# Two changes to a two-block transformer kernel: layer loops written out, and channel sums placed one half lot later

## The chip, the cores and the metric

The kernel runs on one core of a Trainium2 chip, in one launch. The metric is device time in microseconds (us), the median of the runs. The core has a matrix engine (TensorE, PE; its weight loads are shown apart as PEld), three engines for elementwise work (VectorE, DVE; ScalarE, ACT; GpSimd, POOL) and SyncE (SP), which here starts most DMA transfers. Each engine runs its own instruction stream; they meet through semaphores only.

## The reference

Two different transformer blocks of two layers each run one after the other on 512 tokens of width 1024 in fp32. The first has 16 leading meta tokens, so it works on 528.

```python
for l in range(2):                        # first block, 528 tokens
    z = rms_norm(h) @ w_in                # q, k, v, forget logit, a_val, a_gate, sc_b, sc_c, sc_x
    y_attn = forgetting_attention(q, k, v, log_sigmoid(f_logit + b))
    a = a_val * sigmoid(a_gate)
    a = causal_depthwise_conv(a, a_dw_w) + a_dw_b      # 31 taps, 256 channels
    y_conv = silu(layer_norm(a)) @ a_pw_w              # mean and variance over the 256 channels
    y_sc = sc_b * causal_depthwise_conv(sc_c * sc_x, sc_conv_w)   # 3 taps
    h = h + rms_norm(head_rms_norm([y_attn, y_conv, y_sc]) @ w_out)
    h = h + rms_norm((silu(g) * up) @ w_down)          # g, up: causal conv of rms_norm(h) @ w_up
for l in range(2):                        # second block, 512 tokens
    x = x + [stick_breaking, moba, nsa, diff attention](rmsnorm(x) @ w_in) @ w_out
    x = x + square(relu(rmsnorm(x) @ w_up)) @ w_down
```

## The kernel before

Activations stay in SBUF with the features on the 128 partitions and the tokens along the row. Each fp32 operand of a large product is split into a high and a low part, and a product is three matmuls (`product`: L156, L157, L159). Weights come in tiles of 2048 columns into a ring of two slots (SP, L1211 in the input stage). For each lot of weights ScalarE makes the high part (`weight_high`, L140) and VectorE the low part (`weight_low`, L147).

A layer is a chain of stages. Each stage is one `nc.Block`: a program per engine, with a barrier of all engines behind it. Inside, every engine works in the order in which its code is written; only semaphores tie them together. A `Signal` counts per layer, and its `at(layer, n)` gives the value to wait for: `layer * (per_layer * step) + n * step`. The layers of each block are a loop on the chip (`nc.Fori(0, DEPTH)`, L2012 and L3288), so `layer` is a register, and each such wait needs its value worked out in a register first. There are further loops inside the stages, such as TensorE's over lots (L1241, L1713, L241) and those of the helper `in_rounds` (L176) on ScalarE, VectorE and GpSimd.

The change is in the input stage of the first block (`in_stage_a`). TensorE works there through
- 11 lots of branch weights (gates, values, short convolution, forget logit),
- 8 lots of query and key weights, in a loop of 2 × 4 (L1241),
- the channel sums of the long convolution (`channel_sums(acc)`, four matmuls at L1252), which wait for all taps,
- 4 lots of value weights: two pairs, `s` = 0 and 1, each with a first and a second `half` of the 8 contraction steps. For each half, five token tiles of 4 products are accumulated in five PSUM banks (`V_BANKS`); between the pairs stand the channel sums of the squares (`channel_sums(gate)`), and behind them the pointwise product (L1287).

VectorE does the 31 taps of the long convolution on two groups of channels (L1403), spread between the lots, the last 32 of its 62 steps in the loop over query and key lots. Behind the channel sums it centres the result (L1464), does the forget gate's running sum (L1472), the low part of the third value lot, the short convolution (L1481 to L1490), the low part of the fourth, and the scaling by the root (L1502). ScalarE squares the centred result (L1345), makes the high part of the third value lot, copies the values of the first pair out of PSUM (L1309), makes the high part of the fourth, and takes the logarithm, the root and the silu (L1356, L1359, L1364).

The taps' wait is in front of the value lots, so these stand behind it although they don't need the convolution:

```python
pe.wait_ge(dve_step.sem, dve_step.at(layer, M["steps"]["conv"]))
channel_sums(acc)
for s in range(2):
```

At the start of the input stage TensorE adds 2 to its own count of done lots; ScalarE's first weight copy (L140) waits for it.

Of the kernel before, what the change touches and what calls it, by code (L numbers as in the profile page):

```python
# [9 lines left out]

# [18 lines left out]
DEPTH = 2  # L31
# [28 lines left out]
class Signal:  # L60


    def __init__(self, sem, per_layer, step=1):
        self.sem, self.per_layer, self.step = sem, per_layer, step
# [29 lines left out]
class Scope:  # L94


    def __init__(self, nc, ctx):
        self.nc, self.ctx = nc, ctx

    def sb(self, name, shape, dtype=F32):  # L100
        return self.ctx.enter_context(self.nc.sbuf_tensor(name, shape, dtype))

    def parts(self, name, *shape):
# [1064 lines left out]
def in_stage_a(nc, S, G, W, layer, A, M, h):  # L1168
# [5 lines left out]
    act_out, dve_out, dve_step, f_step = S["act_out"], S["dve_out"], S["dve_step"], S["f_step"]  # L1174
# [6 lines left out]
    mm0, QK, V, N_LOTS = 2, 11, 19, 23  # L1181
# [20 lines left out]
    with nc.Block() as block:  # L1202
# [11 lines left out]
        def _(pe):  # L1214
# [33 lines left out]
            def channel_sums(x):  # L1248

                for j in range(2):  # L1250
                    for c, (c0, cn) in enumerate(chunks(TA)):
                        mm = nc.tensor.matmul(ps[:, 6 + c, 0:cn], S["mean256"][:, :], x[:, j, c0:c0 + cn],  # L1252
                                              start=(j == 0), stop=(j == 1))
                mm.then_inc(ln_pe.sem, 1)


            pe.wait_ge(dve_step.sem, dve_step.at(layer, M["steps"]["conv"]))
            channel_sums(acc)
            for s in range(2):
                for half in range(2):  # L1260
                    p = V + 2 * s + half
                    pe.wait_ge(w_lo.sem, w_lo.at(layer, p + 1))
                    for i, (q0, _) in enumerate(K_TILES_A):
                        if half == 0 and (s == 1 or i >= 2):

                            pe.wait_ge(act_out.sem, act_out.at(layer, 15 + i if s else 13 + (i >= 4)))
                            if s == 0:
                                pe.wait_ge(qk_low.sem, qk_low.at(layer, 9 + (i >= 4)))
                        for k in range(4):
                            kk, cols = 4 * half + k, slice(k * 256, (k + 1) * 256)  # L1270
                            mm = product(nc, [ps[:, V_BANKS[i], 0:256]],
                                         tuple(w[:, kk * TA + q0:kk * TA + q0 + P] for w in u_wide),
                                         [(W["hi"][:, p % 2, cols], W["lo"][:, p % 2, cols])],
                                         kk == 0, kk == KD - 1)
                        mm.then_inc(mm_done.sem, 1)
                if s == 0:

                    pe.wait_ge(ln_act.sem, ln_act.at(layer, 2))
                    channel_sums(gate)
# [617 lines left out]
def first_stack(nc, G, A, h):  # L1897

    with ExitStack() as ctx:
# [109 lines left out]
            glu_stage_a(nc, S, G, W, D, layer, A, M, hid, h)  # L2009
            layer_end_a(nc, S, G, layer, A, y, h, col("ffn_post"))  # L2010

        with nc.Fori(0, DEPTH) as layer:  # L2012
            with ExitStack() as whole:
                held = Scope(nc, whole)
                pads = held.sb("y_a", [P, 4 * (TA + TAPS_SHORT - 1) + 4 * TA])
                W = weight_parts(held, "w_a")
                y = part(pads, 0, KD, TA)
                with ExitStack() as inner:
                    mixer(layer, Scope(nc, inner), y, W)
                with ExitStack() as inner:  # L2020
                    glu(layer, Scope(nc, inner), y, pads, W)
# [1130 lines left out]
def second_stack(nc, G, A, h_all, out):  # L3152

    h = h_all[:, :, META:TA]
    with ExitStack() as ctx:
# [129 lines left out]
                             needs=(S["sq_out"], (20 + 8, 20 + 16)), stats=1, free="down_free", bank=4)]  # L3285
            mlp_stage_b(nc, S, G, W, layer, A, ups, downs, col("mlp_g"), u, relu, hid, h)

        with nc.Fori(0, DEPTH) as layer:  # L3288
            with ExitStack() as inner:
                mixer(layer, Scope(nc, inner))  # L3290
            with ExitStack() as inner:
                mlp(layer, Scope(nc, inner))
# [233 lines left out]
```

## Time and profile before

| what | value |
|---|---|
| median of 3 runs | 3087.64 us (3073.48 to 3090.52) |
| the profiled execution: its time, its span | 3083.47 us, 3081.7 us |
| instructions in the profile | 48063 |
| mean granted TensorE clock | 0.949 of full speed |
| first block, layer 0 and layer 1 | 26 to 772 us, 772 to 1523 us |
| second block, layer 0 and layer 1 | 1527 to 2294 us, 2294 to 3073 us |

The span is the time from the first to the last instruction of the profile. "Busy" leaves out register, branch and semaphore instructions; these are shown on an engine's queue (PEldq, DVEq, ACTq) in the views by source line. The granted clock is TensorE's: 1.00 is 2.4 GHz and 0.50 is 1.2 GHz. A row in order of time gives the start, the duration, what ran, and in brackets how long the engine was idle before it and what ended this; a merged row "x8" holds eight records (each of the four matmuls of the channel sums leaves two).

### The profile page before, as it was taken

The page shows a single profiled execution, that of the slowest core. Times are in us where ns is not written, and L with a number is a line of the kernel's source. Part 1 is how long each engine was busy: PE and PEld are TensorE (multiplying, and loading weights), DVE is VectorE, ACT ScalarE, POOL GpSimd, SP SyncE. Part 2 cuts the span into 40 slices and gives each one's busy share as a digit, 9 for nine tenths or more (in the row PEclk, how much of TensorE's full clock was granted, in tenths as well). Part 3 has the DMA queues.
Part 4 walks back from the last instruction along what each step waited for, and adds up shares of the span by engine and source line. Part 5 has one row for each costly group of instructions (what it writes and reads, how often), then busy time and mean ns, then how long its engine had stood idle before and what let it go on. Part 6 is the DMA issues. An engine that isn't in the chain of part 4 may idle for free. (4 is left out here: it accounts for less than half of the span.)

```text
span 3081.7 us, 48063 instructions
## 1 busy us (share of the span) xinstructions
PE 2867.3 (93%) x18250; PEld 2459.6 (80%) x18250; DVE 1435.9 (47%) x2287; ACT 1069.1 (35%) x1486; POOL 236.5 (8%) x210
## 2 busy tenths in 40 slices
PE   7988899999889989999898889999989888999998
PEld 6977899998887789999787556788868754578886
DVE  3633477732563367772333554433433255443343
ACT  3234433322224443332333333422323333343232
POOL 1001300010100120001100022000010001200001
PEclk9989999999998899999899889999999988899999
DMA  3200322222210132222322001222222200122223
GB/s 126 90 28 15 130 82 95 77 95 74 89 69 14 42 117 95 82 91 95 111 100 92 28 1 44 92 96 96 96 88 96 96 28 1 42 82 95 96 96 109
DMA packets 44806, 238.20 MB, mean 77 GB/s; under 512 B 4895, under 2 KB 14751, under 8 KB 21361
## 3 DMA queue, kind: packets, MB, share of 16 engines
q1 hardware_dynamic: 34976, 223.04, 20.9%
q10 hardware_dynamic: 9680, 13.17, 1.3%
q8 instruction: 94, 1.54, 0.2%
q14 instruction: 56, 0.45, 0.0%
HBM read 234.04 MB, written 11.59 MB: 80 GB/s over the span
## 5 line engine op out<-in xcount | busy, mean ns | idle before, releaser
L156 PE MATMUL psum<-u_up_a_hi,w_a_hi 128*128 128x264 f32 x1408 | 378.7, 289 | 19.2 <-DVE u_up_a_lo L1882 15.8
L157 PE MATMUL psum<-u_up_a_lo,w_a_hi 128*128 128x264 f32 x1408 | 374.5, 286 | 0.0
L147 DVE TENSOR_TENSOR w_mlp_b_lo<-ring,w_mlp_b_hi 128x1024 fp32r<-128x1024 f32 x128 | 157.0, 1226 | 330.3 <-ACT w_mlp_b_hi L140 330.3
L147 DVE TENSOR_TENSOR w_a_lo<-ring,w_a_hi 128x1024 fp32r<-128x1024 f32 (+1 forms) x154 | 187.7, 1220 | 227.8 <-ACT w_a_hi L140 225.4
L156 PEld LDWEIGHTS psum<-u_up_a_hi,w_a_hi 128*128 128x128 f32 x1408 | 266.1, 189 | 26.8 <-DVE u_up_a_lo L1882 19.6
L159 PE MATMUL psum<-u_up_a_hi,w_a_lo 128*128 128x264 f32 x1408 | 286.9, 285 | 0.0
L140 ACT ACTIVATE w_a_hi<-ring 128x1024 fp32r<-128x1024 f32 (+1 forms) x154 | 161.4, 1049 | 308.2 <-PE psum L159 303.0
L157 PEld LDWEIGHTS psum<-u_up_a_lo,w_a_hi 128*128 128x128 f32 x1408 | 265.8, 189 | 0.4
L140 ACT ACTIVATE w_mlp_b_hi<-ring 128x1024 fp32r<-128x1024 f32 x128 | 135.6, 1060 | 299.6 <-PE psum L159 298.8
L159 PEld LDWEIGHTS psum<-u_up_a_hi,w_a_lo 128*128 128x128 f32 x1408 | 220.4, 190 | 0.0
L156 PE MATMUL psum<-u_up_b_hi,w_mlp_b_hi 128*128 128x512 f32 x512 | 200.9, 392 | 9.7 <-DVE u_up_b_lo L489 9.7
L157 PE MATMUL psum<-u_up_b_lo,w_mlp_b_hi 128*128 128x512 f32 x512 | 200.6, 392 | 0.0
L159 PE MATMUL psum<-u_up_b_hi,w_mlp_b_lo 128*128 128x512 f32 x512 | 200.3, 391 | 0.0
L156 PE MATMUL psum<-hid_b_hi,w_mlp_b_hi 128*128 128x512 f32 x512 | 199.2, 389 | 0.0
L159 PE MATMUL psum<-hid_b_hi,w_mlp_b_lo 128*128 128x512 f32 x512 | 199.2, 389 | 0.0
L157 PE MATMUL psum<-hid_b_lo,w_mlp_b_hi 128*128 128x512 f32 x512 | 199.2, 389 | 0.0
L156 PE MATMUL psum<-u_in_a_hi,w_a_hi 128*128 128x264 f32 x608 | 167.2, 294 | 28.5 <-DVE u_in_a_lo L1419 19.6
L157 PE MATMUL psum<-hid_a_lo,u_up_a_hi 128*128 128x264 f32 x660 | 173.9, 284 | 0.0
L156 PE MATMUL psum<-hid_a_hi,u_up_a_hi 128*128 128x264 f32 x660 | 173.3, 283 | 0.0
L157 PE MATMUL psum<-u_in_a_lo,w_a_hi 128*128 128x264 f32 x608 | 165.6, 291 | 0.0
L1856 DVE SCALAR_TENSOR_TENSOR y_a<-y_a,cols_a 128x528 f32<-128x528 f32 x176 | 135.3, 769 | 25.3 <-DVE y_a L1856 11.9
L156 PEld LDWEIGHTS psum<-u_in_a_hi,w_a_hi 128*128 128x128 f32 x608 | 118.6, 195 | 31.9 <-DVE u_in_a_lo L1419 21.3
(452 smaller groups left out, 6551.0 us busy)
## 6 DMA issues: line engine op xcount, KB each, us to landing
ring<-in_wup SPq DMA_DIRECT2D x44, 1024.0 KB, 4.8
ring<-in_wup_b SPq DMA_DIRECT2D x32, 1024.0 KB, 4.8
ring<-in_wdown_b SPq DMA_DIRECT2D x32, 1024.0 KB, 4.9
ring<-in_win SPq DMA_DIRECT2D x22, 1024.0 KB, 4.8
ring<-in_wdown SPq DMA_DIRECT2D x32, 704.0 KB, 4.0
ring<-in_win_b SPq DMA_DIRECT2D x12, 1024.0 KB, 4.8
near_copies<-near_rows ACTq DMA_DIRECT2D x2, 4608.0 KB
ring<-in_wout SPq DMA_DIRECT2D x8, 1024.0 KB, 4.8
```

Source lines behind the costliest of these rows:

```text
L140: nc.scalar.activation(W["hi"][:, buf, 0:n], W["tiles"][:, slot, at:at + n], ACT.Copy).then_inc(W["w_hi"].sem, 1)
L147: nc.vector.tensor_tensor(W["lo"][:, buf, 0:n], W["tiles"][:, slot, at:at + n], W["hi"][:, buf, 0:n].bitcast(F32), ALU.subtract).then_inc( ...
L156: nc.tensor.matmul(out[c], a_hi, b_hi, start=start, stop=False)
L157: nc.tensor.matmul(out[c], a_hi, b_lo, start=False, stop=False)
L159: mm = nc.tensor.matmul(out[c], a_lo, b_hi, start=False, stop=stop)
L1856: nc.vector.scalar_tensor_tensor(out=cv[:, j, :], in0=z_pad[:, j, tap:tap + TA], scalar=wcol[tap], in1=cv[:, j, :], op0=ALU.mult, op1=ALU. ...
```

## The change

There are two edits. The layer loops of both blocks become loops of the source: each layer's code is written out, and `layer` is a number. A tile name would then be used twice, so `Scope.sb` adds a number to it. And `channel_sums(acc)` with its wait is placed behind the first half of the first value pair. The other engines' code stays as it is.

```diff
 class Scope:
+    used = collections.Counter()
     def sb(self, name, shape, dtype=F32):
+        self.used[name] += 1
+        name = name if self.used[name] == 1 else f"{name}_{self.used[name]}"
         return self.ctx.enter_context(self.nc.sbuf_tensor(name, shape, dtype))
...
-
-            pe.wait_ge(dve_step.sem, dve_step.at(layer, M["steps"]["conv"]))
-            channel_sums(acc)
             for s in range(2):
                 for half in range(2):
                     p = V + 2 * s + half
+                    if p == V + 1:
+
+                        pe.wait_ge(dve_step.sem, dve_step.at(layer, M["steps"]["conv"]))
+                        channel_sums(acc)
                     pe.wait_ge(w_lo.sem, w_lo.at(layer, p + 1))
...
-        with nc.Fori(0, DEPTH) as layer:      # first block
+        for layer in range(DEPTH):
...
-        with nc.Fori(0, DEPTH) as layer:      # second block
+        for layer in range(DEPTH):
```

TensorE in the input stage, before: the end of the loop over query and key lots, the channel sums (matmuls of `mean`, which is 1/256 everywhere), and the start of the first value pair (its stationary operand is the activation, so the names stand the other way round).

```order
L159 MATMUL psum<-u_in_a_hi,w_a_lo 128x264 x2
L1241 REGISTER_ALU
L1241 COMPARE_AND_BRANCH
L1257 ISA
L1252 MATMUL psum<-arena_a,mean 128x264 [waits dve_step]
L1252 MATMUL psum<-arena_a,mean 128x264 x3
L1262 REGISTER_ALU
L156 MATMUL psum<-w_a_hi,u_in_a_hi 128x256 [waits w_lo_a]
L157 MATMUL psum<-w_a_lo,u_in_a_hi 128x256
```

After, the end of the same loop with what follows it, and the place of the sums 60 matmuls on (lines of the changed kernel are 5 or 6 higher):

```order
L164 MATMUL psum<-u_in_a_hi,w_a_lo 128x264 x2
L1246 REGISTER_ALU
L1246 COMPARE_AND_BRANCH
L161 MATMUL psum<-w_a_hi,u_in_a_hi 128x256 [waits w_lo_a]
L162 MATMUL psum<-w_a_lo,u_in_a_hi 128x256
```

```order
L164 MATMUL psum<-w_a_hi,u_in_a_lo 128x256
L1257 MATMUL psum<-arena_a,mean 128x264 [waits dve_step]
L1257 MATMUL psum<-arena_a,mean 128x264 x3
L161 MATMUL psum<-w_a_hi,u_in_a_hi 128x256 [waits w_lo_a]
L162 MATMUL psum<-w_a_lo,u_in_a_hi 128x256
```

The value lot follows the loop at once, the sums stand between its two halves, and the register instructions in front of the waits are gone.

VectorE at the end of a layer of the first block, before: the last residual additions, the barrier, and the loop's jump back to the input stage.

```order
L580 TENSOR_TENSOR h<-h,y_a 128x528 [waits res_scaled]
L567 UNCONDITIONAL_BRANCH
L2012 REGISTER_ALU [waits barrier_Pool_Activation_PE_DVE_SP_release]
L2012 COMPARE_AND_BRANCH
L3288 UNCONDITIONAL_BRANCH [waits barrier_Pool_Activation_PE_DVE_SP_release]
```

After, the end of layer 0 and the start of layer 1:

```order
L585 TENSOR_TENSOR h<-h,y_a 128x528 [waits res_scaled] x2
L572 UNCONDITIONAL_BRANCH
L1381 UNCONDITIONAL_BRANCH [waits barrier_Pool_Activation_PE_DVE_SP_release]
L1415 MEMSET arena_a 128x2x30
L1416 MEMSET arena_a 128x2x2
```

The jump is gone and the next layer's first operation stands straight behind the barrier. TensorE has 4634 rows in its program before and 8607 now, VectorE 1410 and 1829; the loops inside the stages are kept.

## Rows read from the trace of the kernel before

**Rows 1.** The page: busy time and share of each engine.
```profile
PE 2867.3 (93%) x18250; PEld 2459.6 (80%) x18250; DVE 1435.9 (47%) x2287; ACT 1069.1 (35%) x1486; POOL 236.5 (8%) x210
```

**Rows 2.** TensorE in order of time: start us, us, line, operation, [idle before].
```profile
154.43 0.40 PE L159 MATMUL psum<-u_in_a_hi,w_a_lo 128*128 128x264 f32 x2
...
160.57 3.88 PE L1252 MATMUL psum<-arena_a,mean 128*128 128x264 f32 x8 [5.74 <-DVE arena_a L1403]
...
179.08 1.94 PE L1252 MATMUL psum<-arena_a,mean 128*128 128x264 f32 x8
...
180.66 0.47 PE L156 MATMUL psum<-w_a_hi,u_in_a_hi 128*128 128x256 f32 x1
...
194.94 0.28 PE L159 MATMUL psum<-w_a_hi,u_in_a_lo 128*128 128x256 f32 x1
...
908.35 3.89 PE L1252 MATMUL psum<-arena_a,mean 128*128 128x264 f32 x8 [5.74 <-DVE arena_a L1403]
...
926.74 1.94 PE L1252 MATMUL psum<-arena_a,mean 128*128 128x264 f32 x8
```

**Rows 3.** Stretches: us, busy of PE, PEld, DVE, ACT, POOL, granted clock, DMA.
```profile
160.50:165.60 5.10, 5.03 (x15) 4.20 (x16) 1.12 (x3) 0.36 (x1) 0.00 (x0) 0.50 0.17 72
...
200.30:291.60 91.30, 82.69 (x519) 63.34 (x519) 33.76 (x120) 40.05 (x82) 11.39 (x14) 0.83 0.00 1
...
948.00:1043.20 95.20, 86.94 (x519) 66.99 (x519) 33.70 (x120) 40.04 (x82) 11.41 (x14) 0.78 0.00 1
...
1728.90:1884.90 156.00, 140.72 (x1014) 82.46 (x1014) 84.50 (x282) 56.28 (x89) 28.91 (x24) 0.86 0.00 1
...
2500.50:2663.30 162.80, 147.09 (x1014) 84.95 (x1014) 84.56 (x282) 56.27 (x89) 28.91 (x24) 0.82 0.00 1
```

**Rows 4.** ScalarE and VectorE in order of time, around the moved step.
```profile
155.84 0.59 ACT L1340 ACTIVATE qk_hi<-psum 128x528 f32 x1
...
157.11 0.70 DVE L1453 SCALAR_TENSOR_TENSOR qk_lo<-psum,qk_hi 128x528 f32 x1
...
164.50 1.32 DVE L1464 TENSOR_TENSOR arena_a<-arena_a,psum 128x528 f32<-128x528 f32 x2 [3.98 <-PE psum L1252]
...
172.18 1.06 ACT L140 ACTIVATE w_a_hi<-ring 128x1024 fp32r<-128x1024 f32 x1 [5.68 <-PE psum L159]
```

**Rows 5.** All engines in order of time, at the four input stages' starts.
```profile
25.55 1.04 ACT L1138 ACTIVATE fixed_a<-fixed_a_staged 128x1024 fp32r<-128x1024 f32 x1
...
32.28 0.59 PE L156 MATMUL psum<-u_in_a_hi,w_a_hi 128*128 128x264 f32 x1 [8.05 <-DVE u_in_a_lo L1419]
...
770.48 0.64 ACT L559 ACTIVATE rstd<-rstd 128x528 f32<-128x528 f32 x1
...
774.61 0.11 DVE L1409 MEMSET arena_a<- 128x60 f32 x1 [7.05 <-issue]
...
780.26 0.59 PE L156 MATMUL psum<-u_in_a_hi,w_a_hi 128*128 128x264 f32 x1 [10.54 <-DVE u_in_a_lo L1419]
...
1524.49 1.72 ACTq L2094 DMA_DIRECT2D strips<-near_copies  x1
...
1531.78 0.79 PE L156 MATMUL psum<-u_in_b_hi,w_in_b_hi 128*128 128x512 f32 x1 [10.03 <-DVE u_in_b_lo L2251]
...
2293.88 0.63 ACT L327 ACTIVATE rstd<-rstd 128x512 f32<-128x512 f32 x1
...
2303.64 0.80 PE L156 MATMUL psum<-u_in_b_hi,w_in_b_hi 128*128 128x512 f32 x1 [10.52 <-DVE u_in_b_lo L2251]
```

**Rows 6.** Loop branches by line: count, ns min/median/max, first and last start.
```profile
L2012 PEldq COMPARE_BRANCH  x2: 78/1895/3712, 771.6 to 1523.8; - x2
...
L1713 PEldq COMPARE_BRANCH  x20: 76/212/220, 408.1 to 1374.8; - x20
...
L176 DVEq COMPARE_BRANCH  x52: 49/56/78, 394.9 to 3048.5; - x52
```

**Rows 7.** ScalarE in order of time, layer end: the operation ahead of 770.48.
```profile
769.75 0.70 ACT L556 ACTIVATE rstd<-psum,eps 128x528 f32<-128x528 f32 x1 [1.52 <-PE psum L547]
```

More of the change, by code:

```diff
@@ L13 @@
+import collections
 from contextlib import ExitStack, nullcontext
```

## The prediction

> **What bounds the kernel now.** I read four views: the page for the busy shares, then TensorE's rows in order of time around the moved step, then the stretches with their granted clock, and last the rows on both sides of each stage boundary. In the page TensorE is busy for 93% of the span and no other engine for half of it [rows 1], so an edit is worth what it takes out of TensorE's idle time or gives back of its clock. Two places are touched.
>
> The first is the long convolution of the input stage. TensorE ends its last query/key lot at 154.43 + 0.40 = 154.83 us, waits 5.74 us for VectorE's last tap, computes the channel sums from 160.57 us, and then has value work up to the next channel sums at 179.08 us [rows 2]. It runs at the lower of its two clock levels, 1.2 GHz, from 160.5 to 165.6 us: the stretch shows a granted clock of 0.50 [rows 3]. So the wait is paid twice, as idle time and as slow work behind it. Layer 1 repeats it: wait 5.74 us, sums from 908.35 us, next sums at 926.74 us [rows 2].
>
> The second is the edge between the two layers of each block. From the last operation of the stage ahead to TensorE's first matmul of the input stage there are, in the first block, 32.28 − 26.59 = 5.69 us at layer 0 (the operation starts at 25.55 us and takes 1.04 us) but 780.26 − 771.12 = 9.14 us at layer 1. In the second block they are 1531.78 − 1526.21 = 5.57 us (from the end of a DMA issue of 1.72 us that starts at 1524.49 us) and 2303.64 − 2294.51 = 9.13 us [rows 5]. The work after the boundary is the same; only the later ones are reached by the loop's jump back. TensorE's branch there takes 3.712 us once (taken) and 0.078 us once (loop left) [rows 6].
>
> **The change part by part.** *The sums behind the first half.* The step issues four 264-column matmuls per layer and one wait; nothing else moves, no DMA, and SP's and GpSimd's rows do not hold it. TensorE's row becomes: first half of the first value lots (60 matmuls), wait for the taps, four matmuls, second half. At full clock the four take 180.66 − 179.08 = 1.58 us, and two halves take 194.94 + 0.12 − 180.66 = 14.40 us (lots of the same shape in the second pair, 0.12 us from matmul to matmul) [rows 2]. Each half is then 7.20 us, longer than the 5.74 us that are to be filled: it would end at 162.0 us, when the tap that ended the wait (at about 160.5 us) is 1.5 us old, so the moved wait costs nothing.
>
> Before, from 160.57 to 179.08 us, 18.51 us; at full clock 1.58 + 14.40 = 15.98 us. Gain in layer 0: 5.74 + 18.51 − 15.98 = 8.27 us. In layer 1: 5.74 + (926.74 − 908.35) − 15.98 = 8.15 us. Together 16.4 us. The 2.5 us of clock in each agree with half of the 5.1 us at 0.50 [rows 3].
>
> Can the first half start 5.74 us earlier? Its weights' low part is made in the loop ahead. Its fifth tile writes the bank that the last query/key lot is read from: ScalarE reads it at 155.84 us and VectorE at 157.11 + 0.70 = 157.81 us [rows 4], while the fifth tile is only due at 154.83 + 4 × 1.44 = 160.6 us. Covered by 2.8 us; without this cover the wait would come back before tile 5.
>
> What is queued behind the sums? VectorE's centring starts at 164.50 us now [rows 4]; then it would start with the end of the sums, 162.0 + 1.6 + some 0.3 = 163.9 us, so no later. ScalarE's squares end some 2 us on, at 166 us, and TensorE's next sums need them at 154.83 + 15.98 = 170.8 us: 5 us of room where there were 13. ScalarE's copy of the next weights stands behind those squares. Today it starts at 172.18 us [rows 4], when the first half frees its buffer; then the squares release it at about 166 us, VectorE's low part follows by 168.5 us, and TensorE asks for it at 170.8 + 1.6 = 172.4 us: 4 us of room. From there each step keeps its distance to TensorE's, and the stage's end moves forward whole.
>
> *The layer loops in the source.* Both jumps back go, and layer 1 is entered straight on as layer 0 is: (9.14 − 5.69) + (9.13 − 5.57) = 3.45 + 3.56 = 7.0 us. VectorE shows it too: its first operation of layer 1 starts at 774.61 us, 3.49 us behind ScalarE's last [rows 5]. Inner loops stay loops, and they already jump back without such a stall: TensorE's in the gated unit take 0.076 to 0.220 us, VectorE's 0.049 to 0.078 us over 52 of them [rows 6]. The price is a program for each engine nearly twice as long.
>
> The Trainium skill, "Runtime: NRT & Kernel Launch", Instruction fetch mechanics, says that a taken branch whose target is not in the held window of two 16 KiB pages waits for its code to be fetched. It names no price; the 3.712 us is this case's row. The Trainium skill, "Advanced Engine Details and Errata", Control Flow Timing, gives about 108 ns for a compare-and-branch and speaks against a gain: by it the two jumps are worth an estimated 0.2 us, and the sum would be 16.6 us instead of 23.4 us. The trace bears it out for inner loops and contradicts it for the layer's.
>
> *Waits on constants.* With the layer known, waits outside the inner loops need no register arithmetic. Where the trace shows such a wait it costs nothing: the table operation that starts at 769.75 us and takes 0.70 us is followed, over a wait on a register, 0.03 us later [rows 5, 7]. That is the lower end, 0. The upper end is by the nearest row that bears a price per wait, VectorE's loop branch with at most 0.078 us [rows 6]: if some 100 handoffs of the attention stages lost as much, 7.8 us. A loss has no carrier, since nothing is added. I take 0, as in the row of the wait itself.
>
> *What no row fixes.* The attention stages run the same code in both layers and take different times, as their clock falls differently: 91.3 and 95.2 us in the first block (0.83 and 0.78), 156.0 and 162.8 us in the second (0.86 and 0.82) [rows 3]. The change moves all four in time by 8 to 23 us, so each may land on either figure: −3.9 or +3.9 in the first block, −6.8 or +6.8 in the second, a range of ±10.7 us, middle 0.
>
> **The sum.** 16.4 + 7.0 = 23.4 us. Against the profiled execution, 3083.47 us, that gives 3060 us (span 3081.7 − 23.4 = 3058.3 us, and 1.8 us around it). Its median of runs was 4.2 us higher, 3087.64 us, which gives 3064 us. I forecast 3062 us.
>
> **The rivals.** *A: the jump's price returns.* The fetch is not avoided but shifts to the entry of layer 1, because its code was never loaded before. For it: half of each program is new code. Against it: layer 0's entries are new code too and cost 5.6 us. Then 16.4 us are left: 3083.5 to 3087.6 − 16.4, about 3070 us.
>
> *B: the sums' wait moves instead of going.* If the chain of centring, squares and weights were 5 us longer than worked out, TensorE would wait at the next sums for the 8 us gained, and only the loops' 7.0 us stay: about 3079 us. Against it: the 4 and 5 us of room above, from rows at either end.
>
> *C: slower, by inner loops that no longer stay loaded.* The duplicated code stands at other addresses. If the long loop of the gated unit (9 jumps back per layer, bodies of 24 us) lay so that its start is dropped before the jump, each jump would cost TensorE 3.7 us as the layer's did: 18 × 3.5 = 63 us, and the time 3062 + 63 = 3125 us. From 7 such jumps on (7 × 3.5 = 24.5 us) it eats the gain. Against it: 20 branches there with a maximum of 0.220 us [rows 6], and the bodies keep their length. The Trainium skill's section on instruction fetch, named above, would allow this for a body that leaves the window.
>
> *D: the clock's draw.* All four attention stages on their slow side: the gain shrinks by 10.7 us, to 3073 us.
>
> **How the numbers follow.** Forecast 0.68, A 0.10, B 0.08, C 0.04, D 0.10. A measurement of this kernel tells about 0.5% (15.4 us) from no change, so "faster" ends at 3072.2 us. The forecast gives 0.66 of faster, A half, D half, B none; with some room for what I do not see: faster 0.80, within 0.16, slower 0.04. The range takes in the two scales (3060 and 3064), the upper end of the constants (−7.8), the clock's draw both ways and A and D: 3046 to 3077 us. B's end and C lie outside, about 0.1.
>
> **What would show it.** The wait of 5.74 us at the convolution's sums is gone in both layers, or is under 0.5 us, and no granted clock of 0.50 stands behind it; the next sums start about 16 us behind the last query/key lot, without a new wait. The branch of 3.7 us is absent, and the first matmul of layer 1 comes 5.5 to 6 us behind the stage ahead in both blocks. Wrong would be: a wait for squares or weights in the value lots (B), 9 us at layer 1's entry (A), inner branches above 1 us (C), or attention stages that all take longer (D).

## The result, and the profile after

The changed kernel takes 3052.66 us, the median of 6 runs (3048.62 to 3057.41); the kernel before takes 3081.34 us in 6 runs on the same chip (3073.48 to 3090.52). The ratio is 0.9904, with a 95% interval of 0.988 to 0.9928, so it is faster clear of the noise, by about 1%. The forecast was 3062 us in a range of 3046 to 3077 us. The span fell from 3081.7 to 3055.6 us and the instructions from 48063 to 45807. Lines of the changed kernel are 5 or 6 higher than those of before.

The page of the changed kernel, busy time of each engine: TensorE does the same 18250 matmuls in nearly the same busy time as in [rows 1], in a shorter span.

```profile
PE 2866.0 (94%) x18250; PEld 2463.7 (81%) x18250; DVE 1437.4 (47%) x2287; ACT 1068.1 (35%) x1486; POOL 236.4 (8%) x210
```

TensorE of the changed kernel in order of time, around the moved sums (L1257 now, L161 to L164 are the products). It answers to [rows 2].

```profile
154.05 0.40 PE L164 MATMUL psum<-u_in_a_hi,w_a_lo 128*128 128x264 f32 x2
154.29 0.28 PE L161 MATMUL psum<-w_a_hi,u_in_a_hi 128*128 128x256 f32 x1
...
161.38 1.94 PE L1257 MATMUL psum<-arena_a,mean 128*128 128x264 f32 x8
...
170.26 1.95 PE L1257 MATMUL psum<-arena_a,mean 128*128 128x264 f32 x8
...
894.97 1.94 PE L1257 MATMUL psum<-arena_a,mean 128*128 128x264 f32 x8
...
903.85 1.95 PE L1257 MATMUL psum<-arena_a,mean 128*128 128x264 f32 x8
```

There is no bracket in front of either sum: both waits of 5.74 us are gone, and so is the slow clock behind them, since the first sums take 1.94 us for their eight records, as the second do, instead of 3.88 us. The same in stretches (columns as in [rows 3]): the first half lot, then the sums and the second half.

```profile
154.20:161.30 7.10, 7.10 (x63) 7.10 (x62) 4.62 (x7) 1.56 (x2) 0.00 (x0) 1.00 0.46 148
...
161.38:170.26 8.88, 8.88 (x71) 8.62 (x69) 6.86 (x10) 3.76 (x11) 0.00 (x0) 1.00 0.01 2
```

ScalarE and VectorE behind the sums, which answer to [rows 4]: the squares are made from 164.10 us and end at 164.10 + 1.26 = 165.36 us, 4.9 us ahead of the sums over them, and the copy of the next weights starts at 165.27 us instead of 172.18 us.

```profile
164.10 1.26 ACT L1351 ACTIVATE arena_a<-arena_a 128x528 f32<-128x528 f32 x2 [8.06 <-DVE arena_a L1470]
165.27 1.04 ACT L145 ACTIVATE w_a_hi<-ring 128x1024 fp32r<-128x1024 f32 x1
...
163.36 1.32 DVE L1470 TENSOR_TENSOR arena_a<-arena_a,psum 128x528 f32<-128x528 f32 x2 [3.23 <-PE psum L1257]
...
166.50 1.19 DVE L152 TENSOR_TENSOR w_a_lo<-ring,w_a_hi 128x1024 fp32r<-128x1024 f32 x1
```

The four entries of an input stage, ScalarE's last operation ahead of each and TensorE's first matmul. They answer to [rows 5] (in the second block's first entry the DMA issue on ACTq is the one ahead).

```profile
26.67 1.04 ACT L1143 ACTIVATE fixed_a<-fixed_a_staged 128x1024 fp32r<-128x1024 f32 x1
...
33.23 0.56 PE L161 MATMUL psum<-u_in_a_hi,w_a_hi 128*128 128x264 f32 x1 [7.88 <-DVE u_in_a_lo L1425]
...
759.97 0.64 ACT L564 ACTIVATE rstd<-rstd 128x528 f32<-128x528 f32 x1
...
761.05 0.11 DVE L1415 MEMSET arena_a<- 128x60 f32 x1 [4.58 <-PEq L572]
...
766.15 0.56 PE L161 MATMUL psum<-u_in_a_hi,w_a_hi 128*128 128x264 f32 x1 [6.95 <-DVE u_in_a_lo L1425]
...
1496.14 0.45 ACTq L2100 DMA_DIRECT2D strips<-near_copies  x1
...
1502.42 0.77 PE L161 MATMUL psum<-u_in_b_hi,w_in_b_hi 128*128 128x512 f32 x1 [8.87 <-DVE u_in_b_lo L2257]
...
2264.63 0.63 ACT L332 ACTIVATE rstd<-rstd 128x512 f32<-128x512 f32 x1
...
2270.53 0.76 PE L161 MATMUL psum<-u_in_b_hi,w_in_b_hi 128*128 128x512 f32 x1 [6.66 <-DVE u_in_b_lo L2257]
```

Layer 1 is entered in 766.15 − 760.61 = 5.54 us in the first block (9.14 before) and in 2270.53 − 2265.26 = 5.27 us in the second (9.13 before): 3.60 + 3.86 = 7.46 us. Layer 0's entries take 5.52 and 5.83 us, about as before. VectorE's first operation of layer 1 comes 0.44 us behind ScalarE's last, where it was 3.49 us. The layer's branch is gone from the trace.

How the branch of before got onto the path takes a second look, since TensorE itself had nothing to do in its 3.7 us. ScalarE's first weight copy of the stage waits until TensorE has added to its count (L1232). The branch starts at 771.6 us and takes 3.712 us, so it ends at 775.3 us, and the copy follows:

```profile
775.52 1.06 ACT L140 ACTIVATE w_a_hi<-ring 128x1024 fp32r<-128x1024 f32 x1 [4.40 <-PEq L1232]
```

VectorE's low part, and with it TensorE's first matmul at 780.26 us, stand behind this copy. In the changed kernel the copy starts at 761.11 us, 0.5 us behind ScalarE's last operation. TensorE's branch is not the whole delay: ScalarE and VectorE, too, went on only at 774.4 us before, so a quick branch on TensorE alone would have won about 1 us (an estimate, 775.5 − 774.5). And what goes on meanwhile shows in the DMA queues: from 771.5 to 775.3 us, while TensorE stands in the branch, the queues of instructions move five packets.

```profile
q14 instruction: 4, 0.03, 2.9%
q8 instruction: 1, 0.02, 2.1%
```

At the second block's jump (2294.9 to 2298.6 us) they move three. In the same stretches of the changed kernel, 760.8 to 764.6 us and 2265.4 to 2269.1 us, they move none.

The attention stages and the short stick-breaking ahead of the second block's attention, in stretches; the first four answer to [rows 3].

```profile
191.60:282.60 91.00, 83.10 (x519) 63.78 (x519) 33.82 (x120) 39.99 (x82) 11.43 (x14) 0.83 0.00 1
925.20:1017.20 92.00, 84.08 (x519) 64.46 (x519) 34.03 (x120) 40.05 (x82) 11.43 (x14) 0.81 0.00 1
1702.80:1856.30 153.50, 138.16 (x1014) 83.12 (x1014) 85.45 (x282) 56.13 (x89) 28.83 (x24) 0.87 0.00 1
2470.80:2635.20 164.40, 148.92 (x1014) 87.64 (x1014) 85.63 (x282) 56.23 (x89) 28.83 (x24) 0.81 0.00 1
1641.20:1702.80 61.60, 46.33 (x240) 26.59 (x240) 28.04 (x61) 20.24 (x33) 0.00 (x0) 0.84 0.20 68
```

The stage of the last row took 58.2 us at a clock of 0.91 before:

```profile
1670.70:1728.90 58.20, 43.30 (x240) 24.61 (x240) 28.03 (x61) 20.24 (x33) 0.00 (x0) 0.91 0.21 73
```

### Where the 26 us of the span are

From barrier to barrier of the two traces, in us; "written out" and "moved" are the two single edits of the experiments below.

| stage | before | after | moved | written out |
|---|---|---|---|---|
| input, first block, layer 0 | 173.6 | 163.8 | 164.1 | 171.1 |
| input, first block, layer 1 | 176.7 | 164.4 | 168.6 | 169.8 |
| gated unit, layers 0 and 1 | 410.5, 410.5 | 408.3, 408.6 | 410.5, 410.5 | 408.4, 408.7 |
| input, second block, layer 1 | 147.9 | 144.0 | 147.7 | 144.0 |
| attention, first block | 91.2, 95.2 | 91.0, 92.0 | 91.4, 90.3 | 87.8, 87.8 |
| stick-breaking, second block | 58.2, 57.9 | 61.5, 61.5 | 59.5, 59.6 | 61.4, 61.4 |
| attention, second block | 156.1, 162.9 | 153.5, 164.4 | 162.8, 159.2 | 150.5, 164.4 |

Input stages give 9.9 + 12.3 + 3.9 us, the gated unit 4.1 us. The stages of the last three rows together lose some 2.3 us, and the other stages differ by less than 1.5 us each.

### The profile page after: what moved, and what is told of

Its sections match the earlier page's. It is cut to its first block and busy times, and to the rows that moved or that the text cites. A ratio compares the mean times of both kernels' runs of the same rounds, so it can differ in the third digit from the quotient of the medians.

```text
span 3055.6 us, 45807 instructions
## 1 busy us (share of the span) xinstructions
PE 2866.0 (94%) x18250; PEld 2463.7 (81%) x18250; DVE 1437.4 (47%) x2287; ACT 1068.1 (35%) x1486; POOL 236.4 (8%) x210
## 5 line engine op out<-in xcount | busy, mean ns | idle before, releaser
L161 PE MATMUL psum<-u_up_a_hi,w_a_hi 128*128 128x264 f32 x1408 | 378.6, 289 | 15.6 <-DVE u_up_a_lo L1888 15.4
L164 PE MATMUL psum<-u_up_a_hi,w_a_lo 128*128 128x264 f32 x1408 | 287.0, 285 | 0.0
L161 PEld LDWEIGHTS psum<-u_up_a_hi,w_a_hi 128*128 128x128 f32 x1408 | 266.1, 189 | 22.4 <-issue 14.6
L164 PEld LDWEIGHTS psum<-u_up_a_hi,w_a_lo 128*128 128x128 f32 x1408 | 220.5, 190 | 0.0
L161 PE MATMUL psum<-u_up_b_hi,w_mlp_b_hi 128*128 128x512 f32 x512 | 201.6, 394 | 9.7 <-DVE u_up_b_lo L494 9.7
L164 PE MATMUL psum<-u_up_b_hi,w_mlp_b_lo 128*128 128x512 f32 x512 | 200.9, 392 | 0.0
L161 PE MATMUL psum<-hid_b_hi,w_mlp_b_hi 128*128 128x512 f32 x512 | 199.3, 389 | 0.0
L164 PE MATMUL psum<-hid_b_hi,w_mlp_b_lo 128*128 128x512 f32 x512 | 199.2, 389 | 0.0
L161 PE MATMUL psum<-u_in_a_hi,w_a_hi 128*128 128x264 f32 x608 | 166.9, 293 | 23.4 <-DVE u_in_a_lo L1425 15.0
L161 PE MATMUL psum<-hid_a_hi,u_up_a_hi 128*128 128x264 f32 x660 | 173.3, 283 | 0.0
L1862 DVE SCALAR_TENSOR_TENSOR y_a<-y_a,cols_a 128x528 f32<-128x528 f32 x176 | 135.3, 769 | 24.3 <-DVE y_a L1857 6.1
L152 DVE TENSOR_TENSOR w_in_b_lo<-ring,w_in_b_hi 128x1024 fp32r<-128x1024 f32 x48 | 59.3, 1235 | 173.8 <-ACT w_in_b_hi L2195 173.8
```

What stands on the lines that cost most here:

```text
L152: nc.vector.tensor_tensor(W["lo"][:, buf, 0:n], W["tiles"][:, slot, at:at + n], W["hi"][:, buf, 0:n].bitcast(F32), ALU.subtract).then_inc( ...
L161: nc.tensor.matmul(out[c], a_hi, b_hi, start=start, stop=False)
L164: mm = nc.tensor.matmul(out[c], a_lo, b_hi, start=False, stop=stop)
L1862: nc.vector.scalar_tensor_tensor(out=cv[:, j, :], in0=z_pad[:, j, tap:tap + TA], scalar=wcol[tap], in1=cv[:, j, :], op0=ALU.mult, op1=ALU. ...
```

## The experiments

### One edit at a time

First the sums' move alone: the changed kernel with both layer loops back on the chip.

```diff
-        for layer in range(DEPTH):
+        with nc.Fori(0, DEPTH) as layer:      # both blocks
```

> The sums behind the first half of the first value lots, with the layer loops left on the chip. Theory (two separate gains that add up): the wait of 5.74 us per layer and the slow clock behind it go, 16.4 us, so the ratio to the kernel before is about 0.9947; the two jumps of 3.7 us stay, and an iteration of the gated unit's long loop stays at 23.95 us. Rival (the written-out layers are what makes room for the moved sums, as fewer register instructions stand ahead of the waits): a new wait shows at the next channel sums or in the value lots, and less than 10 us are gained.

Measured: 3068.09 us, ratio 0.9953 (0.9926 to 0.9981). The sums stand at full clock without a wait, close to the ratio of 0.9947 that was expected. The layers' branches are back: TensorE's taken one takes 3.918 us in the first block (the row below) and 3.456 us in the second.

```profile
L1257 PE MATMUL psum<-arena_a,mean x32: 386/386/387, 162.3 to 912.3; 128*128 128x264 f32 x32
...
L2018 PEldq COMPARE_BRANCH  x2: 67/1992/3918, 763.8 to 1502.5; - x2
```

Then the loops alone: the changed kernel with the sums at their old place.

```diff
+            pe.wait_ge(dve_step.sem, dve_step.at(layer, M["steps"]["conv"]))
+            channel_sums(acc)
             for s in range(2):
...
-                    if p == V + 1:
-                        pe.wait_ge(dve_step.sem, dve_step.at(layer, M["steps"]["conv"]))
-                        channel_sums(acc)
```

> The layers written out, with the channel sums at their old place. Theory: 7.0 us from the two entries, some 4 us from the gated unit's long loop (23.95 us an iteration before, 23.73 us in the changed kernel), ratio about 0.9965; the wait of 5.74 us and the clock of 0.50 behind it stay in both layers. Rival (the jump's price returns at the entry of layer 1, or the long loop is faster for the place of its code alone and not for this part): first matmul of layer 1 about 9 us behind the stage ahead, ratio 0.999 to 1.001.

Measured: 3067.86 us, ratio 0.9953 (0.9931 to 0.9974); the expected 0.9965 lies inside the interval. The wait is there, 5.74 us to the hundredth, in both layers. Layer 0:

```profile
158.99 3.66 PE L1257 MATMUL psum<-arena_a,mean 128*128 128x264 f32 x8 [5.74 <-DVE arena_a L1407]
...
176.68 1.95 PE L1257 MATMUL psum<-arena_a,mean 128*128 128x264 f32 x8
```

What follows: by the whole times the edits are additive as far as these can tell. 0.9953 × 0.9953 = 0.9906, and both together measured 0.9904. The table shows most of each gain in its own stages: the move's in the first block's input stages (9.5 and 8.1 us), the loops' in the two entries of layer 1 and, which I had not forecast, in the gated unit, which falls by 2 us per layer only where the layers are written out.

Stage by stage the traces add up less well. The loops alone also shorten the first block's input stages by 2.5 and 6.9 us (3.6 us of the latter are the entry), while on top of the move they give only 0.3 and 4.2 us. Most of the difference is the clock: in the trace of the loops alone the wait of 5.74 us is followed by 17.69 and 17.71 us up to the next sums instead of 18.51 and 18.39 us, and behind the wait for the forget logit in layer 1 the clock did not fall at all.

```profile
843.20:851.20 8.00, 7.94 (x65) 7.94 (x66) 2.95 (x5) 5.63 (x7) 0.00 (x0) 1.00 0.35 126
```

So what the slow clock adds to one and the same wait is not a fixed sum: behind 5.74 us it was 1.7 us in this trace (17.69 − 15.98) and 2.5 us in that of the kernel before.

### The wait's idle time and the clock behind it

The kernel before, with 44 matmuls of no use in front of the taps' wait, so that TensorE is busy there and the rest of the program stays as it is.

```diff
+            pe.wait_ge(w_lo.sem, w_lo.at(layer, V + 1))
+            for n in range(44):
+                nc.tensor.matmul(ps[:, V_BANKS[0], 0:256], u_wide[0][:, n % 4 * TA:n % 4 * TA + P],
+                                 W["hi"][:, V % 2, n % 4 * 256:(n % 4 + 1) * 256], start=True, stop=True)
             pe.wait_ge(dve_step.sem, dve_step.at(layer, M["steps"]["conv"]))
```

> The kernel before with 44 matmuls of the first value lot's operands in front of the wait for the taps; what they write is overwritten, the output is the same. They take 44 x 0.12 = 5.3 us of the wait of 5.74 us. Theory (half of what the move gave beyond the wait is TensorE's clock): the sums still start at 160.6 us, but at the full level, and the next sums come 16.0 us behind them instead of 18.5 us; 5 us in all, ratio 0.998. Rival (the slow stretch is the price of the wait's end or of the changed operands, not of idle time): the stretch behind stays at 0.50, and the ratio is 1.000.

Measured: 3079.78 us, ratio 0.9988 (0.9961 to 1.0015), so the whole time can't tell it from no change. The stages can: the two input stages take 171.1 and 173.4 us, 2.5 and 3.3 us less than before. TensorE in order of time, and the stretch behind the wait:

```profile
154.08 5.36 PE L1259 MATMUL psum<-w_a_hi,u_in_a_hi 128*128 128x256 f32 x44
...
159.99 2.05 PE L1252 MATMUL psum<-arena_a,mean 128*128 128x264 f32 x8 [0.54 <-DVE arena_a L1408]
...
176.07 1.95 PE L1252 MATMUL psum<-arena_a,mean 128*128 128x264 f32 x8
...
160.00:176.00 16.00, 16.00 (x128) 15.74 (x129) 8.90 (x13) 4.10 (x11) 0.00 (x0) 1.00 0.05 22
```

The sums still wait for the tap, but from them to the next sums it is 16.08 us instead of 18.51 us. In layer 1 it is 16.08 us instead of 18.39 us. So 2.4 and 2.3 us of each 8.2 us were not idle time but slow work behind it, as the prediction split it.

### The sums half a pair later still

The sums behind the whole first value pair, directly ahead of the sums of the squares. It measures the room that the squares and the weights have.

```diff
-                    if p == V + 1:
-                        pe.wait_ge(dve_step.sem, dve_step.at(layer, M["steps"]["conv"]))
-                        channel_sums(acc)
...
                 if s == 0:
+                    pe.wait_ge(dve_step.sem, dve_step.at(layer, M["steps"]["conv"]))
+                    channel_sums(acc)
```

> The changed kernel with the sums one half lot later still, behind the whole first pair. Theory (the room behind the moved sums is real and finite): TensorE then waits for centring and squares, some 2.4 to 3 us ahead of the next sums, and about 0.6 us for the weights of the second pair: 3 to 3.5 us per layer, 6 to 7 us more than the changed kernel, ratio to the kernel before about 0.9925. Rival (there is no room already, the changed kernel is at its edge): each us of delay costs one, 7.2 us per layer or 14 us in all, ratio about 0.995. Rival two (the sums are off the path altogether): no difference to the changed kernel, 0.9904.

Measured: 3057.81 us, ratio 0.9915 (0.9886 to 0.9943). This interval holds the theory's 0.9925 and also the 0.9904 of "no difference", so the whole time decides only against 0.995. The stages decide more. The two input stages take 166.6 and 166.2 us, 2.8 and 1.7 us more than after the change, and TensorE's rows say why:

```profile
168.00 1.95 PE L1257 MATMUL psum<-arena_a,mean 128*128 128x264 f32 x8
...
172.03 2.05 PE L1257 MATMUL psum<-arena_a,mean 128*128 128x264 f32 x8 [2.08 <-ACT arena_a L1349]
...
174.36 0.39 PE L161 MATMUL psum<-w_a_hi,u_in_a_hi 128*128 128x256 f32 x1 [0.28 <-DVE w_a_lo L152]
```

From the sums to the squares' release it is 172.03 − 168.00 = 4.03 us. In the changed kernel 170.26 − 161.38 = 8.88 us lie between the two sums, so the room there is 8.88 − 4.03 = 4.85 us. The prediction had 5 us. From the first value matmul to the second sums it is 18.2 us in both layers instead of 15.97 us, and behind them TensorE needs 0.6 and 1.7 us more to the end of the stage. That is 2.9 and 3.9 us against the 3 to 3.5 us expected; layer 1's stage is only 1.7 us longer because the clock ahead of the value lots fell less in this trace (1.00 behind the wait for the forget logit, 0.68 in the changed kernel's). This is the wait of rival B made to happen; half a pair of lots keeps it away.

### The next wait of the same kind

In the changed kernel the largest wait left in the input stage, behind TensorE's first matmul, is TensorE's for the forget logit's bank, ahead of the query and key lots. This version asks for it one lot later, behind the first lot that doesn't need the bank; TensorE's loop over these lots is written out for it.

```diff
-            pe.wait_ge(dve_out.sem, dve_out.at(layer, 5))
...
-            with pe.Fori(0, 2) as it:
+            for it in range(2):
...
+                    if it == 0 and j == 1:
+                        pe.wait_ge(dve_out.sem, dve_out.at(layer, 5))
+                        pass_waits(pe, S)
```

> The changed kernel with one more wait of the same kind put off: TensorE's wait for VectorE's reading of the forget logit stands in front of the second query/key lot (which reuses that bank) instead of the first, and TensorE's loop over these lots is written out. The changed kernel waits 3.64 us there in each layer and runs 3.4 to 6.8 us behind it at 1.2 GHz. Theory (what a wait of TensorE costs is its length and half of the slow stretch behind it): 3.6 + 1.7 to 3.4 us per layer, 10 to 14 us in all, ratio to the kernel before about 0.9865. Rival (the taps on VectorE, which end each of these lots' chain, set the pace, so that TensorE arrives earlier and waits longer at the taps): the wait comes back in front of the channel sums, and the gain is under 4 us, ratio about 0.9895.

Measured: 3040.86 us, ratio 0.9845 (0.9802 to 0.9887), 11.8 us under the changed kernel where 10 to 14 us were expected. Its 6 runs (3023.61 to 3041.84 us) are all below the 6 of the changed kernel (3048.62 to 3057.41 us). The input stages take 158.4 us in both layers, 5.4 and 6.1 us less. From TensorE's waits in layer 0's input stage: the changed kernel has the one below, and this version has none longer than 0.6 us behind the entry.

```profile
PE psum L161 <- issue: 3.6, 1, 3.6
```

```profile
PE psum L161 <- POOL u_in_a_lo L1523: 0.6, 2, 0.5
```

The wait of 3.6 us is gone and no other took its place. Here too about 2 us come from the clock (5.4 and 6.1 us less the 3.6 us of the wait): behind the wait the changed kernel runs 8 us at 0.79 in layer 0 and at 0.68 in layer 1, this version 15 us and more at 1.00. Two edits stand in this version, the later wait and TensorE's loop written out. They were not run apart; the wait and the clock leave no more than some 0.3 us for the loop.

```profile
105.70:113.70 8.00, 7.99 (x53) 7.99 (x54) 2.17 (x4) 4.30 (x6) 0.00 (x0) 0.79 0.31 121
```

```profile
100.00:115.00 15.00, 15.00 (x125) 15.00 (x124) 10.21 (x15) 7.72 (x9) 0.00 (x0) 1.00 0.22 72
```

### Why the gated unit gained

First attempt: only the gated unit stands in a loop of one pass whose register is the layer.

```diff
-            glu_stage_a(nc, S, G, W, D, layer, A, M, hid, h)
+            with nc.Fori(layer, layer + 1) as on_chip:
+                glu_stage_a(nc, S, G, W, D, on_chip, A, M, hid, h)
```

> The changed kernel with the gated unit's stage inside a loop on the chip of one pass, whose register stands for the layer, so that its waits are worked out in registers again as in the kernel before; all else stays written out. Theory (register instructions around the waits are what made the long loop faster): its iterations take 23.95 us again instead of 23.73 us, the stage 410.5 us instead of 408.4 us, and 4 us are lost in all, ratio about 0.992. Rival (the place of the code, or the clock): 23.73 us stay, ratio 0.9904.

Measured: 3057.9 us, ratio 0.9917 (0.989 to 0.9945), gated unit 408.4 and 408.7 us. It decides nothing: the loop of one pass left no register for the layer, and the rows show the same register instructions as in the changed kernel (at TensorE's loop branch one of 53 ns and one of 32 ns per pass, where the kernel before has 133 and 36 ns). The theory was not put to the test.

Second attempt, from the other side: instead of adding register work, take the rest of it away. VectorE's long loop over up-lots is written out, the other engines' stay.

```diff
-            in_rounds(dve, rounds, step)
+            for it in range(rounds):
+                step(it, it == rounds - 1)
```

> The changed kernel, with VectorE's long loop of the gated unit (the rounds over up-lots) written out in the source, so that VectorE needs no register instruction there at all; TensorE's and ScalarE's loops stay. Theory (the 2.1 us per layer that the gated unit gained came from fewer register instructions between VectorE's dependent operations, on the chain that ends at TensorE's one gap per round): the gap ahead of the first tap falls from about 0.25 to 0.15 us, a round of 23.73 us falls by 0.1 to 0.25 us until the gap of 0.31 us is gone, and the gated unit takes 406 to 407.5 us instead of 408.4. Rival (the gain came from TensorE's or ScalarE's own register instructions): rounds of 23.73 us and 408.3 to 408.6 us as before. A stage longer than 409 us would say that VectorE now waits for its code. Whole kernel by the theory 3049 us, by the rival 3053 us, each within the clock's draw.

Measured: 3054.64 us, ratio 0.9901 (0.9868 to 0.9934), the same as the changed kernel as far as whole times tell; but the gated unit takes 406.4 us in both layers, 1.9 and 2.2 us less, inside the 406 to 407.5 us expected. VectorE's taps by line, before, after, and in this version (count | busy us, mean ns of one | idle time ahead of all of them, and what ended the gaps above 0.15 us):

```profile
L1856 DVE SCALAR_TENSOR_TENSOR y_a<-y_a,cols_a 128x528 f32<-128x528 f32 x176 | 135.3, 769 | 25.3 <-DVE y_a L1856 11.9 <-DVE y_a L1851 11.8
L1851 DVE TENSOR_SCALAR y_a<-y_a,cols_a 128x528 f32<-128x528 f32 x88 | 43.6, 496 | 20.0 <-DVE y_a L1843 19.3
```

```profile
L1862 DVE SCALAR_TENSOR_TENSOR y_a<-y_a,cols_a 128x528 f32<-128x528 f32 x176 | 135.3, 769 | 24.3 <-DVE y_a L1857 6.1 <-DVE y_a L1862 6.1
L1857 DVE TENSOR_SCALAR y_a<-y_a,cols_a 128x528 f32<-128x528 f32 x88 | 43.6, 495 | 16.8 <-DVE y_a L1849 10.9
```

```profile
L1862 DVE SCALAR_TENSOR_TENSOR y_a<-y_a,cols_a 128x528 f32<-128x528 f32 x176 | 135.4, 769 | 6.2
L1857 DVE TENSOR_SCALAR y_a<-y_a,cols_a 128x528 f32<-128x528 f32 x88 | 43.6, 495 | 3.1
```

The taps last the same. In front of a tap that reads the one before it, VectorE stood idle for 25.3 / 176 = 0.144 us before, 24.3 / 176 = 0.138 us after and 6.2 / 176 = 0.035 us in this version. (The releasers named behind the arrow would tell another story, 11.9 + 11.8 us against 6.1 + 6.1 us. But only gaps above 0.15 us are counted there, and these gaps lie at 0.15 us.) What stood there are the register instructions that work out the addresses and counts. In one case of the kernel before, a tap ends at 424.58 us, the register instruction, which waits for this tap, runs from 424.62 to 424.69 us, and the next tap starts at 424.74 us. With both lines the idle time is 45.3, 41.1 and 9.3 us.

The taps are on a chain: taps, product, ScalarE's high part of `hid`, a load of ScalarE's table (1.28 us), the copy of the next weights, VectorE's low part, TensorE. In the kernel before, TensorE's only wait in this loop is the end of that chain (layer 0, 8 times about 0.2 us); in the changed kernel the same view shows none.

```profile
L156 PE MATMUL psum<-u_up_a_hi,w_a_hi 128*128 128x264 f32 x658 | 175.0, 286 | 1.6 <-DVE w_a_lo L147 1.6
```

TensorE's branch at the end of its loop gives the pass, first and last of a layer, before, after, and in this version; the last row is the stretch of nine passes in this version (columns as in [rows 3]):

```profile
L1713 PEldq COMPARE_BRANCH  x10: 76/208/220, 408.1 to 623.1; - x10
```

```profile
L1719 PEldq COMPARE_BRANCH  x10: 76/208/216, 399.0 to 612.3; - x10
```

```profile
L1719 PEldq COMPARE_BRANCH  x10: 76/208/216, 399.5 to 611.0; - x10
```

```profile
399.50:611.00 211.50, 211.50 (x1731) 211.50 (x1730) 164.70 (x219) 79.74 (x88) 0.00 (x0) 1.00 0.25 86
```

That is 215.0 / 9 = 23.89 us before, 213.3 / 9 = 23.70 us after, 211.5 / 9 = 23.50 us in this version. The two steps are equal by chance. In the first, VectorE's idle time falls by 4.2 us in 22 rounds, 0.19 us a round, and the pass falls by as much. In the second it falls by 31.8 us, 1.4 us a round, and the pass only by 0.2 us, because then TensorE is busy for the whole 211.50 us and nothing is left to gain there. TensorE's own loop is the same in the last two, so its register work is not the cause of the second step. For the first step the register instructions of all three engines changed at once. That VectorE's made the gain is the likeliest reading of a wait on VectorE's low part that went and of two falls of the same 0.19 us; ScalarE's share on the same chain was not shown apart.

Last, the two together: the late forget wait, and VectorE's and ScalarE's long loops written out.

> The changed kernel with the late wait for the forget logit (the earlier experiment that took 3040.9 us), and with the long loop of the gated unit written out in the source for VectorE and ScalarE both. Theory: input stages of 158.4 us as in that experiment, gated unit 405.5 to 407 us (by VectorE, ScalarE adds at most the same again through the copy ahead of the late weight copy), whole kernel about 3036 to 3038 us. Rival (register instructions of TensorE alone): gated unit 408.3 us and 3041 us. A second rival: ScalarE's part alone counts, then this kernel gains and the one with VectorE's loop alone does not.

Measured: 3035.28 us, ratio 0.9841 (0.9807 to 0.9875), the lowest median of all and just under the 3036 to 3038 us expected; input stages 158.4 us, gated unit 406.4 us in both layers. ScalarE's part adds nothing (406.4 us without it), as TensorE had no idle time left there. Against the version with the late wait alone, 0.9845, the whole times don't tell a gain; the stage does.

## Why the prediction was right, and where it was off

**The sums' move: right, in mechanism and size.** It forecast 5.74 us of idle time and some 2.5 us of clock per layer, the next sums 15.98 us behind the last query/key lot, and 5 us of room at the squares. From the first value matmul behind that lot, at 154.29 us, it is 170.26 − 154.29 = 15.97 us. Measured from the start of that lot's last row, the second sums came 179.08 − 154.43 = 24.65 us later before and 170.26 − 154.05 = 16.21 us after: 8.44 us gained against 8.27 us. In layer 1 it is 8.32 us against 8.15 us. The filled wait gave the clock's part alone (18.51 − 16.08 = 2.43 us) and the later place gave the room (4.85 us). VectorE's centring started at 163.36 us (forecast 163.9 us), and the weights' low part ended at 166.50 + 1.19 = 167.7 us (168.5 us worked out), 4.1 us before TensorE asks for it at 170.26 + 1.58 us (forecast 4 us). The first block's input stages fell by 9.9 and, without the entry's 3.6 us, 8.7 us. The rest, 1.4 and 0.4 us, lies ahead of the moved step and is no merit of it: in layer 0 the 8 us behind the forget wait ran at 0.62 before (below) and at 0.79 after, which is 1.4 us of work. The forecast had no term for it.

```profile
104.90:112.90 8.00, 8.00 (x43) 8.00 (x44) 1.99 (x3) 3.88 (x5) 0.00 (x0) 0.62 0.31 124
```

**The jumps: right.** 7.46 us against 7.0 us. Rival A had the price return at layer 1's first entry; those entries take 5.54 and 5.27 us, no more than layer 0's. New code met straight on costs nothing that the rows show; the jump back over a whole layer costs TensorE 3.5 to 3.9 us (six records in three traces, 3.456 to 3.918 us). Rival C did not come either: TensorE's branches in the gated unit stay at 0.216 us at most, and no branch anywhere in the changed kernel's trace takes more than 0.24 us. The prediction has one thing wrong that cost it nothing: each engine's program was to be nearly twice as long, which holds for TensorE (4634 to 8607 rows) but not for VectorE (1410 to 1829). The Trainium skill, "Runtime: NRT & Kernel Launch", Instruction fetch mechanics, says that prefetch is sequential and that a taken branch out of the held window breaks it; both halves agree with these rows and with the instruction packets seen during the branch. The Trainium skill's other rule, "Advanced Engine Details and Errata", Control Flow Timing, with about 108 ns for a compare-and-branch, is near what the inner branches show (0.076 to 0.216 us in TensorE's loop of the gated unit). For the two jumps it would have given an estimated 0.2 us where the entries show 7.46 us; there the measurement decides against it.

**Waits on constants: the term that was mis-sized.** I took 0 and kept 7.8 us as the upper end. It is 2.2 + 1.9 = 4.1 us, all of it in the gated unit. I had read the price at one wait of ScalarE's. There the register instruction waits for nothing and ran at 769.76 us, while the operation ahead of it was still running. In front of a tap the register instruction itself waits for the tap before, so it stands between the two, and the idle time is 0.14 us each; this costs kernel time only where the chain reaches TensorE. The rows for it were in the trace of before (25.3 + 20.0 us of idle time in front of those lines), and I had not looked at VectorE inside the gated unit because it isn't the bound there. The upper end of 7.8 us was sought at handoffs of the attention stages, where the clock's draw would hide it; whether they lost or gained by it stays open.

**The clock's draw: right in kind, one stage missed.** I counted the four attention stages (±10.7 us); these gave 0.3, 3.2, 2.6 and −1.5 us, a gain of 4.6 us, which goes with the granted clock and with no edited code: luck. The stick-breaking stages ahead of the second block's attention do it too, and lost 3.3 and 3.6 us, at a clock of 0.84 instead of 0.91. Rival D, all on the slow side, did not come. The loops alone show how far the draw goes: their trace has both attention stages of the first block at 87.8 us, below either figure that the prediction allowed. Over all ten traces the same code took 87.8 to 95.9 us, 57.9 to 61.5 us and 150.5 to 164.6 us in these three places.

**The sum.** Forecast 23.4 us; the span shows 26.1 us. The moved sums gave 8.4 + 8.3 us and the jumps 7.5 us, 24.2 us in all; the clock ahead of the sums 1.8 us and the register work 4.1 us; the draw in the attention and stick-breaking stages and small pieces took 4.0 us back. That the span comes so near the forecast is therefore in part luck: a term put at 0 and the draw nearly cancel. By medians it is 3081.34 − 3052.66 = 28.7 us. The changed kernel is 9.3 us below the forecast and inside the range. Of these, 5.3 us are gain beyond the 23.4 us, and 4.1 us are the kernel before, for which the forecast stood on 3062 + 23.4 = 3085.4 us and whose median of 6 runs is 3081.34 us. The range held the ends of its terms one by one and not together: 7.8 us of constants and a lucky draw of 10.7 us would have given 3041.5 us, below its 3046 us.

## What to carry to other kernels

Where the bound engine waits for a late producer, put independent work of its own in front of the wait, as long as the wait and no longer: the idle time goes and the slow clock behind it too, here about 2.4 us on top of 5.74 us (1.7 us in another trace). Then look for the next such wait and for the chain behind the moved step, and check that this chain's room is longer than the step. An outer loop whose body is far larger than its inner ones can cost microseconds per pass at its jump (3.6 and 3.9 us here), and register work between dependent small operations can cost on a chain of an engine that is busy for less than half the time. It costs there only as long as the bound engine still waits for that chain.

## What the runs showed of the hardware that I had not expected

- A register instruction that waits for VectorE's operation ahead showed as 0.138 to 0.144 us of idle time in front of the next one, though it is itself recorded as 57 to 64 ns. Without it the idle time was 0.035 us (6.2 us over 176 taps).
- A loop's jump back over a whole layer cost TensorE 3.712 and 3.636 us in the trace of before and 3.918 and 3.456 us in that of the moved sums, while GpSimd's, ScalarE's, SyncE's and VectorE's records of that branch were 0.03 to 0.06 us long. ScalarE and VectorE were late all the same: their next instruction stands at 774.4 us, 2.8 to 2.9 us behind their branches, where GpSimd's and SyncE's follow within 0.3 us. So the record of a branch does not hold its whole price on every engine.
- Straight code of a whole second layer was entered without a stall, and packets of the queues of instructions even fell, from 94 to 88 on one queue and from 56 to 38 on the other.
